# Moving the second layer's conditioning projection into the first layer's recurrence

## What is computed

```python
mod_p = (jax.nn.silu(c_ctx) @ w_ada[l] + b_ada[l])[None, None, :]
mod_s = (jax.nn.silu(c) @ w_ada[l] + b_ada[l])[:, None, :]
...
sh1, sc1, g1, sh2, sc2, g2 = jnp.split(mod, 6, axis=-1)
h = rmsnorm(x, lp["norm1"]) * (1 + sc1) + sh1
u = h @ lp["w_in"]
...                       # convolution, Fourier and RWKV-7 branches, merged by gates
x = x + g1 * (merged @ lp["w_o"])
h = rmsnorm(x, lp["norm2"]) * (1 + sc2) + sh2
x = x + g2 * ffn(h)       # dense SwiGLU in layer 0, top-2-of-8 experts in layer 1
```

## Time and profile before

| what | value |
|---|---|
| median of three runs | 2049.8 us |
| time of the profiled execution | 2049.8 us |
| its span on the core | 2048.0 us |
| TensorE busy (PE) | 1830.1 us, 89% |
| VectorE busy (DVE) | 1118.5 us, 55% |
| ScalarE busy (ACT) | 867.9 us, 42% |
| GpSimd busy (POOL) | 476.1 us, 23% |
| HBM read | 310.53 MB, 153 GB/s over the span |

### The profile page before, as it was taken

One profiled execution on the slowest core, in us unless ns is written; L12 is line 12 of the kernel. 1 busy time (PEld: TensorE's weight loads), 2 busy tenths in 40 slices (PEclk: granted clock), 3 DMA queues, 4 the chain that ended last, 5 costly groups with the idle time before them and its releaser, 6 DMA issues.

```text
span 2048.0 us, 40551 instructions
## 1 busy us (share of the span) xinstructions
PE 1830.1 (89%) x16456; PEld 1619.7 (79%) x16456; DVE 1118.5 (55%) x1609; ACT 867.9 (42%) x1273; POOL 476.1 (23%) x362
## 2 busy tenths in 40 slices
PE   4798979899979999979886989997799999999997
PEld 3796868787879999979685978787677877777875
DVE  0465777543231210046467773322678877788876
ACT  2435242332343443244523223233466665667654
POOL 0460000243446666547000014333000000000000
PEclk8999989999999999989998989998799999999998
DMA  9346340132424444424712003332678877788760
GB/s 308 96 134 215 120 157 9 29 127 95 134 83 124 124 124 144 139 71 125 227 57 63 4 4 103 113 103 74 246 272 307 296 257 263 267 299 307 263 234 31
DMA packets 225012, 314.75 MB, mean 154 GB/s; under 512 B 15584, under 2 KB 169574, under 8 KB 224742
## 3 DMA queue, kind: packets, MB, share of 16 engines
q1 hardware_dynamic: 217856, 306.22, 45.7%
q10 hardware_dynamic: 7014, 6.44, 1.1%
HBM read 310.53 MB, written 2.10 MB: 153 GB/s over the span
## 4 chain that ended last, share of the span: by engine, by line
PE 80%; DVE 12%; ACT 3%; issue 2%; DMA 2%; ACTq 1%; DVEq 0%; SPq 0%
PE bank L562 78%; PE bank L559 2%; DVE S L1661 1%; DMA ring<-in_w_ada 1%; DVE cvT L1591 1%; DVE tmp L1606 1%; DVE hT L1458 1%; DVE rs L1453 1%; DVE U L1689 1%; DMA xin<-in_x_sample 0%; DVE hT L1465 0%; DVE xT L1484 0%; DVE St L1707 0%; DVE e_w_rest L178 0%; DVE yT L1779 0%
## 5 line engine op out<-in xcount | busy, mean ns | idle before, releaser
L1971 POOL TENSOR_TENSOR weights_rest<-ring,weights_rounded 128x512 fp32r<-128x512 f32 x344 | 461.5, 1343 | 618.9 <-ACT weights_rounded L1158 618.4
L178 DVE TENSOR_TENSOR e_w_rest<-e_raw,e_w_rounded 128x1024 fp32r<-128x1024 f32 (+1 forms) x324 | 351.7, 1133 | 46.0 <-ACT e_w_rounded L1394 38.7
L1158 ACT ACTIVATE weights_rounded<-ring 128x512 fp32r<-128x512 f32 x344 | 215.7, 630 | 378.6 <-PE bank L562 372.4
L1394 ACT ACTIVATE e_w_rounded<-e_raw 128x1024 fp32r<-128x1024 f32 (+1 forms) x324 | 312.5, 989 | 92.9 <-PE bank L562 86.7
L562 PE MATMUL bank<-h_rounded,weights_rounded 128*128 128x384 f32 x688 | 233.5, 339 | 31.4 <-DVE h_rest L1499 31.4
L562 PE MATMUL bank<-h_rest,weights_rounded 128*128 128x384 f32 x688 | 232.5, 338 | 0.0
L562 PE MATMUL bank<-h_rounded,weights_rest 128*128 128x384 f32 x688 | 232.2, 338 | 0.0
L562 PE MATMUL bank<-e_w_rounded,hG_rounded 128*128 128x512 f32 (+1 forms) x432 | 163.9, 379 | 15.3 <-DVE hG_rest L1929 14.3
L562 PE MATMUL bank<-e_w_rounded,hG_rest 128*128 128x512 f32 (+1 forms) x432 | 161.5, 374 | 0.0
L562 PE MATMUL bank<-e_w_rest,hG_rounded 128*128 128x512 f32 (+1 forms) x432 | 161.0, 373 | 0.0
L562 PEld LDWEIGHTS bank<-h_rounded,weights_rounded 128*128 128x128 f32 x688 | 131.2, 191 | 34.0 <-issue 33.2
(11 more groups left out here) (280 smaller groups left out, 3437.0 us busy)
## 6 DMA issues: line engine op xcount, KB each, us to landing
ring<-in_w_ada SPq DMA_DIRECT2D x96, 512.0 KB, 6.2
e_raw<-in_moe_w_down SPq DMA_DIRECT2D x90, 512.0 KB, 5.0
ring<-in_w_in SPq DMA_DIRECT2D x88, 512.0 KB, 4.7
e_raw<-in_moe_w_gate SPq DMA_DIRECT2D x72, 512.0 KB, 6.0
e_raw<-in_moe_w_up SPq DMA_DIRECT2D x72, 512.0 KB, 7.0
e_raw<-in_moe_w_gate SPq DMA_DIRECT2D x36, 384.0 KB, 5.6
e_raw<-in_moe_w_up SPq DMA_DIRECT2D x36, 384.0 KB, 4.0
ring<-in_ffn_w_gate SPq DMA_DIRECT2D x22, 512.0 KB, 4.8
```

Source lines behind the costliest of these rows:

```text
L178: eng.tensor_tensor(wl, e_raw[n % E_RAW][:, 0:kn * w], wr.bitcast(F32), ALU.subtract).then_inc(s("e_rest"), 1)
L1158: a(w_parts[n % NSLOT][0], raw, ACT.Copy).then_inc(*E.up("rounded_ready", *key))
L1394: a(e_w[n % E_PARTS][0][:, 0:kn * w], e_raw[n % E_RAW][:, 0:kn * w], ACT.Copy).then_inc(s("e_rounded"), 1)
L1971: pool.tensor_tensor(wl, raw, wr.bitcast(F32), ALU.subtract).then_inc(*E.up("rest_ready", *key))
```

## The change

Layer 1's whole matrix is worked off within layer 0's recurrence. Layer 0's list grows from 24 to 40 units, layer 1's becomes empty. To hold them, layer 0 gets more places: one unit ahead of each of the levels 2, 3 and 4 in both directions, and two in place of one in the state steps of direction 1. In layer 1 the state steps of direction 0 have one place in place of two. Layer 1's three groups are copied, turned and turned into modulation vectors together, near the end of layer 0's gates; the same work for two groups in layer 1's direction 1 is gone. The load order of the ring follows.

```diff
-        ada_at = {(l, g): cut(f"ada{l}_{g}", o + 512 * (g - 1) if g else used["adas"][0], 512)
+        ada_at = {(l, g): cut(f"ada{l}_{g}", o + 512 * (g - 1) if (l, g) in ((0, 1), (0, 2)) else used["adas"][0] + 512 * g, 512)
...
-            add_ada(l, range(4, 12))
             if l + 1 < DEPTH:
-                add_ada(l + 1, range(4))
+                add_ada(l, range(4, 12))
+                add_ada(l + 1, range(12))
...
-                parts_left = [(l, i) for i in range(4, 12)] + [(l + 1, i) for i in range(4 if l + 1 < DEPTH else 0)]
+                parts_left = [(0, i) for i in range(4, 12)] + [(1, i) for i in range(12)] if l == 0 else []
...
                         meanwhile(3)
-                        ada_turn(l, (1, 2))
+                        if l == 0:
+                            ada_turn(0, (1, 2))
                         meanwhile(2)
...
                     for lev in range(1, LEVELS + 1):
+                        if l == 0 and 1 < lev < LEVELS:
+                            meanwhile(1)
...
-                        meanwhile(2 if d == 0 else 1)
+                        meanwhile(2 if l == 0 else 1)
...
                 if l + 1 < DEPTH:
-                    ada_turn(l + 1, (0,))
+                    ada_turn(l + 1, range(3))
```

More of the change, by code:

```diff
@@ L1268, in _ @@
                         exps(1)
-                        ada_copies(l, (1, 2))
+                        if l == 0:
+                            ada_copies(0, (1, 2))
                     for cp in range(NCP):
@@ L1342, in _ @@
                             act.wait_ge(*drained("gup", l, i))
-                        ada_copies(l + 1, (0,))
+                        ada_copies(l + 1, range(3))
                     if b_ == 2 and m > 0:
@@ L1653, in _ @@
                         prep(1)
-                        modulation(l, (1, 2))
+                        if l == 0:
+                            modulation(0, (1, 2))
                     for cp in range(NCP):
@@ L1798, in _ @@
                 if l + 1 < DEPTH:
-                    modulation(l + 1, (0,))
+                    modulation(l + 1, range(3))
                 residual(lambda m: ("o", l, m), l, 16, 1)
```

## The result

The changed kernel is slower. It took 2068.21 us (median of 6 runs, 2062.51 to 2072.82) against 2050.36 us of the kernel before on the same chip, a ratio of 1.0082 with a 95% interval of 1.0060 to 1.0104. The prediction said 2056.5 us with a range up to 2066: right in its sign, and too small: +6.7 us forecast, +17.9 us measured. The profiled execution took 2062.35 us with a span of 2060.5 us; it is a little shorter than the shortest of the six, so its trace holds 12.5 us of the 18.

The account below looks back on a forecast made before the run. TensorE was taken to bound the kernel, with 80% of the chain of waits. Terms 5.6 + 4.0 - 1.0 - 6.5 + 0 + 1.4 + 2.3 + 0.9 = +6.7 us on 2049.8 gave 2056.5 us, range 2045 to 2066.

Parts of the forecast that it names:

- What bounds the kernel: Whole kernel: 80% of the chain of waits on TensorE; "issue" is TensorE out of instructions, caused by ring traffic.
- Fills replaced by units, units in the levels: Both layers: swapping fills and units costs 0; six units in layer 0's levels cost 6 x 0.94 = +5.6 us.
- New issue gaps in layer 0: Layer 0, both directions: loads behind the added units starve TensorE of instructions, +4.0 us.
- starvation: Rival, chance 0.12: every burst in layer 0's levels gives a full gap, six at 2.96 us, total 2071 us.
- State steps and Y: Layer 0's direction 1: three more units lie beside VectorE's adding of taps, 0 (-2.1 to +1.8 us).
- Layer 1's levels, -6.5: Layer 1's direction 0: without ring traffic the levels take 34.35 and 33.9 us like others, not 40.9: -6.5 us.
- Layer 1's steps, -1: Layer 1's direction 0, state steps with Y: losing three units and the traffic gives -1 us (-1.7 to 0).
- Ahead of direction 0 in layer 1, 0: Before layer 1's direction 0: 0.6 us to be won without block waits, offset by a lower clock from idling: 0.
- The wait at layer 0's turn, +1.4: Layer 0, start of direction 1: one unit now stands behind the wait for a bank's copy, not under it: +1.4 us.
- The turn gone from layer 1, +2.3: Layer 1's direction 1: removing the turn leaves TensorE idle, so the tok transposes run at lower clock: +2.3 us (0 to +3.5).
- The turns at layer 0's end, +0.9: End of layer 0: eight more transposes, less their overlap, cost +0.9 us (0.7 to 1.5).
- rule of the Trainium skill: Instruction fetch is mostly hidden; by it, new gaps and layer 1's level gain from old ones would be nothing.

Follow-up runs that it names:

- e2: Changed kernel with the loads issued right behind the six level units cut to one of 128 rows: 2058.31 us, ratio 1.0031 to the kernel before.
- e3: Changed kernel with loads of recurrence units from the eleventh on cut to one of 128 rows: 1981.61 us, to be read as 2043.8 since routing changed.
- e4: Kernel before with loads from the eleventh unit of each layer's recurrence on cut to one of 128 rows: 2042.58 us, ratio 0.9948.
- e9: Kernel before with the rotation of PSUM banks 0 to 3 moved on by two at layer 1's start and its direction 1: 2047.44 against 2051.08 us.
- e8: Changed kernel with the last two of five fills at the start of layer 1's direction 1 held behind ScalarE's second exponential: 2067.85 us, ratio 1.0100.
- e11: Changed kernel with the last four of five fills at the start of layer 1's direction 1 held behind ScalarE's third exponential: 2060.48 us, ratio 1.0040.
- e7: Changed kernel without its six level units; the last seven units run one after the other at the end of layer 0's recurrence: 2061.19 us, ratio 1.0059.
- e5: Kernel before with the two units ahead of direction 0's levels turned into fills in both layers, units sliding later: 2047.95 against 2050.10 us, ratio 0.9989.
- e6: Kernel before with layer 1's 16 units in TensorE's waits, layer 0 one unit a step, fills ahead of levels: 2038.71 against 2050.10 us, ratio 0.9946.
- e10: e6 with the bank rotation also moved on by two in layer 1's direction 0: 2038.13 us, ratio 0.9943 to the kernel before.

## Why the prediction was wrong in its size

*What bounds the kernel*: right. The rule "issue is TensorE out of instructions, and the cause is ring traffic" was read from four gaps and is shown by e2 and e3, and by the packets of the instruction queue.

*Fills replaced by units, units in the levels*: right; 3.5 and 2.7 us against e4 where 2.8 each were booked.

*New issue gaps in layer 0*, "so I take 1.5 us a direction for the three together ... +4.0 us": **this is the step that failed.** Gaps in the levels went from 1.23 to 5.55 us in direction 0 and from 0 to 5.55 us in direction 1, +9.9 us, the sums of the chain rows above. Of these, about 6.1 us lie behind the six single units, 1.0 us each against 0.5 us assumed (0.82 to 1.55 us at five of them, none at the sixth), and 3.65 us behind the new pair of direction 1, against the 1.0 us booked in its levels. All that traffic costs the levels, their length less that of e3 or e4, is 6.2 and 8.0 us now and was 1.8 and -0.4 us before: +12.8 us where 4.0 were booked. The levels grew by 19.0 us in all, to 43.1 and 45.5 us, where 9.6 us and levels of 38 to 42 us were forecast. I had argued that the single bursts are half as long as those behind the seen gaps. But with a block due every 3.4 us and bursts behind the single units of 3.6 to 5.4 us every 8 to 10 us, hardly a burst misses one; the prediction had this fact and used it only for its rival.

The rival "starvation" had the mechanism right, with a chance of 0.12, and its 2071 us are near the measured 2068.2. Its price was not right: it booked 2.96 us a single burst, three times the gap measured, and the pair and the steps, where it added nothing, make up for part of that. Its total is partly luck. The microsecond of low clock that it booked behind each gap isn't there in direction 0 (granted clock 1.00 over the levels, with gaps up to 1.55 us), nor in e9 behind a gap of 2.85 us; behind the gap of 3.65 us it is (0.60 over 3.2 us).

*State steps and Y*, "I take 0" (-2.1 to +1.8): wrong too, by +3.3 and +4.3 us for direction 1 in the two profiles. It was judged by direction 0 of the same layer. The same load doesn't fix these steps: with two units each they took 37.0 to 41.3 us in direction 1 of the changed kernel, e2, e8 and e11, but 34.4 us in e7; without traffic (e3) 33.9 us. The granted clock sorts the 56 stretches of steps (14 profiles, four each): at 1.00 they took 32.4 to 33.2 us, at 0.95 33.4 to 34.8 us (36.3 and 37.1 with gaps of 2.75 and 4.7 us), at 0.90 to 0.91 34.9 to 37.2 us, at 0.79 to 0.87 36.7 to 41.3 us. In direction 1, before the change, in e3 and now:

```profile
342.39:377.37 34.98, 27.83 (x584) 24.98 (x578) 26.87 (x52) 1.78 (x3) 0.00 (x0) 0.90 0.01 3
349.92:383.85 33.93, 29.09 (x775) 26.08 (x771) 26.87 (x52) 1.78 (x3) 0.00 (x0) 0.95 0.17 51
365.19:403.53 38.34, 32.12 (x775) 28.36 (x770) 26.87 (x52) 1.79 (x3) 0.00 (x0) 0.87 0.58 181
```

So the +3.3 us are a gap of 2.41 us and a lower clock. Why the clock is lower in direction 1 I haven't settled.

*Layer 1's levels, -6.5*: the size was right (-6.9), the cause half wrong. With the old rotation and gaps of at most 0.73 us these levels took 36.7 to 37.2 us at a clock of 0.95 (e4, e5, e6), with the new one and gaps of at most 0.4 us 33.4 to 34.4 at 1.00 (the changed kernel, e2, e3, e7, e8, e10, e11). So about 4 us are traffic and about 3 us the bank rotation, which the change moved by accident.

*Layer 1's steps, -1*: -2.9 and 0.0 in the two profiles; direction 1's, not counted at all, -4.3 and -3.2, though nothing was changed in it. Other profiles have 32.4 to 37.6 us there with fills alone, at clocks from 1.00 down to 0.82, so this is scatter of the clock and not the change.

*Ahead of direction 0 in layer 1, 0*: 47.1 to 45.8 us from `ksq` to the first inverse, -1.3, and 45.8 in all kernels of this kind but e3 (46.7).

*The wait at layer 0's turn, +1.4*: the stretch grew from 37.3 to 38.8 us twice, but it is 37.2 in e3, which keeps the unit behind the wait and has no traffic. So the unit itself costs nothing there, and the traffic does; of the 1.5 us, a gap of 0.74 us in the `pair` products is seen. The size was right by chance. (In e7 the stretch is 37.1 us, but there the unit stands ahead of the wait, as before the change.)

*The turn gone from layer 1, +2.3*: +2.6 and +3.1, and e11 shows the cause, the clock.

*The turns at layer 0's end, +0.9*: can't be told: the stretch from layer 0's last `sf` to `ksq` is 0.3 and 0.5 us longer, and scatters by more (602.7 to 604.2 us in kernels whose turns are the old ones).

Of the rule of the Trainium skill ("Runtime: NRT & Kernel Launch", Instruction fetch mechanics) that fetching is mostly hidden: without ring traffic the runs agree (e3, 0.3 us of gaps), with it they don't, 15.0 us between 150 and 415 us.

## What to carry to other kernels

A load that is free in bandwidth isn't free where an engine runs through small instructions: look in the chain for "issue" behind bursts of DMA, and count how many blocks of instructions fall due during a burst. Work that brings its own traffic belongs where the engine waits for something else, even if it then waits for its data there: with units placed so the kernel was 11 us faster than before (e6); the changed kernel, with six of them among the levels, was 18 us slower. Before a gap in the schedule is filled or an item is taken out of one, see what else the item did: here it kept the clock up and set which buffer comes next.

## What the hardware showed that I had not expected

Behind a single burst of 1 MB (3 us of loads) TensorE lost up to 1.55 us in the first profile and up to 1.90 us in the others, behind two units (2 MB) 0.84 to 3.65 us. In the changed kernel's levels the gaps came after 125 or 126 matmuls or twice as many. Cutting the loads to one row took nearly all of it away, in both kernels (0.3 and 0.6 us left in layer 0's recurrence).

The steps of a recurrence with hardly any traffic and no gap over 0.42 us took anything from 32.4 us at a granted clock of 1.00 to 37.6 us at 0.82 (layer 1's direction 1 in the changed kernel and in e10, with the same fills).

A total's scatter may come from the gaps: on one chip the kernel before ran from 2044.1 to 2060.8 us in 25 executions, and e4, with most of the traffic gone, from 2040.0 to 2047.2 us in ten. That the gaps fall differently from one execution to the next is seen for the changed kernel alone, which has two profiles (11 gaps and 15).

A rotation of four banks by two, with no instruction changed, was worth about 3 us in one stretch (2.8 us in e10 against e6, where the granted clock over it rose from 0.95 to 1.00, with one profile of each; 3.7 us in e9, not all of it the rotation's).
